# The multiplier of a gated recurrence, computed as (1 + a) times the root of -tanh(y/2) instead of through a reciprocal

## The reference

```python
r = sigmoid(gate_r(x)); i = sigmoid(gate_i(x))
log_a = -LRU_C * r * softplus(-lam)
a = exp(log_a)
mult = sqrt(-expm1(2.0 * log_a))          # the root of 1 - a^2
u = mult * (i * x)
h = scan(h = a * h + u)                   # along the 256 tokens
y_lru = h * gelu(u_g)
```

## Time and profile before

| | us |
|---|---|
| median of 3 runs | 942.52 |
| lowest and highest of them | 936.86, 943.32 |
| the profiled execution, its own time | 943.4 |
| its span, from the first to the last instruction | 941.6 |

### The profile page before, as it was taken

One profiled execution on the slowest core, in us unless ns is written; L12 is line 12 of the kernel. 1 busy time (PEld: TensorE's weight loads), 2 busy tenths in 40 slices (PEclk: granted clock), 3 DMA queues, 4 the chain that ended last, 5 costly groups with the idle time before them and its releaser, 6 DMA issues.

```text
span 941.6 us, 13290 instructions
## 1 busy us (share of the span) xinstructions
PE 811.3 (86%) x5425; PEld 644.0 (68%) x5425; DVE 506.0 (54%) x826; ACT 380.0 (40%) x629; POOL 44.4 (5%) x108
## 2 busy tenths in 40 slices
PE   6989997896686776659999997799999999999975
PEld 5967786763343332329989875487787999999854
DVE  5786547411110030055936988945677666666655
ACT  5563647210100100046456655535445544444444
POOL 5000020010101101000000000000000000000000
PEclk9998998998987889779999997989999999999988
DMA  9941181399999999995417452055554566665001
GB/s 285 374 153 45 46 334 46 139 409 422 422 422 420 420 422 421 410 333 170 149 64 302 160 202 89 1 201 179 179 179 134 185 193 196 189 191 200 11 0 45
DMA packets 75950, 205.81 MB, mean 219 GB/s; under 512 B 5720, under 2 KB 48896, under 8 KB 63600
## 3 DMA queue, kind: packets, MB, share of 16 engines
q1 hardware_dynamic: 67406, 150.44, 44.7%
q0 software_dynamic: 8480, 54.49, 14.3%
q10 hardware_dynamic: 2, 0.00, 0.0%
HBM read 203.87 MB, written 1.05 MB: 218 GB/s over the span
## 4 chain that ended last, share of the span: by engine, by line
PE 62%; DMA 16%; DVE 14%; ACT 4%; issue 2%; SPq 0%; POOL 0%; ACTq 0%; DVEq 0%
DMA big<-in_w_up 16%; PE ps L1938 8%; PE ps L1939 8%; PE ps L1940 8%; PE ps L1741 8%; PE ps L1743 7%; PE ps L1742 7%; PE ps L2052 4%; DVE WL L1069 2%; PE ps L2031 1%; DVE XT L1558 1%; DVE WL L1061 1%; DVE big L1600 1%; ACT WH L622 1%; PE ps L2066 1%
## 5 line engine op out<-in xcount | busy, mean ns | idle before, releaser
L1069 DVE TENSOR_TENSOR WL<-big,WH 128x1024 fp32r<-128x1024 f32 x154 | 186.8, 1224 | 111.8 <-ACT WH L622 110.2
L622 ACT ACTIVATE WH<-big 128x1024 fp32r<-128x1024 f32 x154 | 160.7, 1054 | 89.0 <-PE ps L1940 88.5
L1741 PE MATMUL ps<-XH,WH 128*128 128x256 f32 (+1 forms) x640 | 187.5, 293 | 1.0 <-DVE WL L1061 0.7
L1743 PE MATMUL ps<-XH,WL 128*128 128x256 f32 (+1 forms) x640 | 183.1, 286 | 0.0
L1742 PE MATMUL ps<-XL,WH 128*128 128x256 f32 (+1 forms) x640 | 183.1, 286 | 0.0
L1741 PEld LDWEIGHTS ps<-XH,WH 128*128 128x128 f32 x640 | 123.7, 193 | 6.6 <-issue 4.5
L2052 PE MATMUL ps<-big 128*32 128x256 f32 x1024 | 77.8, 470 | 55.1 <-DMA big<-in_w_gate 33.3
L1742 PEld LDWEIGHTS ps<-XL,WH 128*128 128x128 f32 x640 | 123.8, 194 | 0.8
L1743 PEld LDWEIGHTS ps<-XH,WL 128*128 128x128 f32 x640 | 123.6, 193 | 0.0
L2052 PEld LDWEIGHTS ps<-big 128*32 128x32 f32 x1024 | 42.8, 135 | 92.0 <-issue 81.9
L1938 PE MATMUL ps<-WH,XH 128*128 128x512 f32 x240 | 96.6, 402 | 5.6 <-DVE WL L1069 2.1
(11 more groups left out here) (399 smaller groups left out, 1091.7 us busy)
## 6 DMA issues: line engine op xcount, KB each, us to landing
big<-in_w_in SPq DMA_DIRECT2D x35, 1024.0 KB, 9.2
big<-in_w_gate SPq DMA_DIRECT2D x16, 1024.0 KB, 17.1
big<-in_w_up SPq DMA_DIRECT2D x16, 1024.0 KB, 18.2
big<-in_w_gate POOLq DMA_DIRECT2D x16, 1024.0 KB, 19.4
big<-in_w_up POOLq DMA_DIRECT2D x16, 1024.0 KB, 20.1
big<-in_w_down SPq DMA_DIRECT2D x16, 1024.0 KB, 18.6
big<-in_w_down POOLq DMA_DIRECT2D x16, 1024.0 KB, 21.2
big<-in_w_mlp_up SPq DMA_DIRECT2D x16, 1024.0 KB, 5.5
```

The costliest lines, as they stand in the source:

```text
L622: s.activation(dst, src, ACT.Copy).then_inc(ev("unit_high"), 1)
L1069: v.tensor_tensor(dst, src, h.bitcast(F32), ALU.subtract).then_inc(ev("unit_split"), 1)
L1741: mm(o, h, rh, start=first, stop=False, skip_group_check=skip)
L1743: return mm(o, l, rh, start=False, stop=last, skip_group_check=skip)
```

## The change

The reciprocal form is taken out. Tanh gets y/2 through its scale. DVE no longer computes the eight chunks of L1557 to L1559; instead, in steps 30 to 33, it multiplies the gated input by 1 + a, two chunks at a time. ACT's Sqrt of -t follows the Gelu immediately, in steps 33 and 34, and what comes after on DVE stands five steps earlier: the product with the root in steps 35 to 38, the scans in 39 to 42, the gated outputs in 40 to 43. No other engine's stream changes.

```diff
-                    s.activation(half_of(zc, k - 27), half_of(zx, k - 27), ACT.Tanh).then_inc(ev("tanh_done"), 1)
+                    s.activation(half_of(zc, k - 27), half_of(zx, k - 27), ACT.Tanh, scale=0.5)\
+                        .then_inc(ev("tanh_done"), 1)
...
-                if k in (38, 39):
-                    act.wait_ge(ev("one_minus_a2"), 4 * (k - 37))
-                    s.activation(half_of(zc, k - 38), half_of(zc, k - 38), ACT.Sqrt).then_inc(ev("mult_ready"), 1)
+                if k in (33, 34):
+                    s.activation(half_of(zc, k - 33), half_of(zc, k - 33), ACT.Sqrt, scale=-1.0)\
+                        .then_inc(ev("mult_ready"), 1)
...
-                if 29 <= k < 37:
-                    c = k - 29
-                    dve.wait_ge(ev("tanh_done"), 1 + c // 4)
-                    th_, xt = zc[:, c, :], XT[:, 0, 0:S]
-                    chain(v.tensor_scalar(xt, th_, -1.0, 1.0, ALU.mult, ALU.add))
-                    chain(v.reciprocal(xt, xt))
-                    v.scalar_tensor_tensor(out=th_, in0=th_, scalar=-2.0, in1=xt, op0=ALU.mult, op1=ALU.mult)\
-                        .then_inc(ev("one_minus_a2"), 1)
-                    dve.wait_ge(ev("one_minus_a2"), c + 1)
-                if 40 <= k < 44:
-                    q = k - 40
+                if 30 <= k < 34:
+
+                    q = k - 30
+                    dve.wait_ge(ev("a_ready"), 1 + q // 2)
+                    dve.wait_ge(ev("gated_input"), 4)
+                    v.scalar_tensor_tensor(out=two(zi, q), in0=two(zx, q), scalar=1.0, in1=two(zi, q), op0=ALU.add,
+                                           op1=ALU.mult).then_inc(ev("one_plus_a"), 1)
+                if 35 <= k < 39:
+                    q = k - 35
                     dve.wait_ge(ev("mult_ready"), 1 + q // 2)
-                    dve.wait_ge(ev("gated_input"), 4)
+                    dve.wait_ge(ev("one_plus_a"), 4)
                     v.tensor_tensor(two(zi, q), two(zi, q), two(zc, q), ALU.mult).then_inc(ev("lru_input"), 1)
-                if 44 <= k < 48:
-                    if k == 44:
+                if 39 <= k < 43:
+                    if k == 39:
                         dve.wait_ge(ev("lru_input"), 4)
-                        dve.wait_ge(ev("a_ready"), 2)
-                    for c in (2 * (k - 44), 2 * (k - 44) + 1):
+                    for c in (2 * (k - 39), 2 * (k - 39) + 1):
                         v.tensor_tensor_scan(out=zc[:, c, :], data0=zx[:, c, :], data1=zi[:, c, :], initial=0.0,
                                              op0=ALU.mult, op1=ALU.add).then_inc(ev("scanned"), 1)
-                    if k > 44:
-                        gated_output(k - 45)
-            gated_output(3)
+                if 40 <= k < 44:
+                    gated_output(k - 40)
             dve.wait_ge(ev("lru_done"), 4)
```

## The result

Over twelve runs of each, the changed kernel has a median of 934.49 us (933.05 to 937.94) against 942.09 (936.86 to 943.68). The ratio of the runs is 0.9930, with a 95% interval of 0.9916 to 0.9943: 6.6 us less, between 5.4 and 7.9. (The medians alone are 7.6 us apart, the means of the twelve 6.5.) In a second measurement, six runs against ten, it was 0.9929 (0.9904 to 0.9954). The forecast was 937.3 and a saving of 5.2 us, within 1%, in a range of 931.5 to 941.0.

The account below looks back on a forecast made before the run. PE, busy 86% of the span, waits for DVE's reciprocal steps in the token units and for a late first mask. Savings of 2.99 and 2.18 us sum to 5.2, taking the median 942.52 to 937.3, range 931.5 to 941.0.

Parts of the forecast that it names:

- What bounds the kernel: Token units: PE needs 21.96 us per eight units if nothing is late; DVE's reciprocal steps made the first half 2.99 longer.
- Point 1, the stalls: Token units: PE's three stalls on DVE's splits vanish, saving 2.99 us, with bounds of about 2.1 and 3.0.
- The sign named for DVE's time: Sign that the forecast is right: DVE's time over the whole 16 token units falls by about 17 us.
- Point 2, the scans: Steps 39 to 43: DVE falls about 1.6 us behind, covered by 5.9 to spare; cost nothing, at most 1.6 without cover.
- Point 3, ACT: Around units 36 to 38: the moved roots and table load cost nothing, since the smaller slack is 4.0 us.
- Point 4, the mask: Stage end: first mask starts 0.55 us behind the scores instead of 2.73, saving 2.18, bounds 1.9 and 2.7.
- The clock: PE's pause before the attention shrinks from 4.31 to about 2.1 us; whether the clock still falls was open, counted as nothing.
- the two terms: The forecast's two savings: 2.99 us from PE's stalls and 2.18 from the first mask, together 5.2 us.
- Rival A: Clock stays up over the shorter pause: 1.8 us in attention rounds, about 2 in the unit behind; 933.5 us; chance 0.15.
- B: Only one of the two terms comes, as stalls move elsewhere or the mask waits for something else: about 940 us; chance 0.11.
- C: Clock stays at 1.2 GHz through all the attention and first units behind: 6.1 us lost against 5.2 saved, 943.4; chance 0.04.
- D: The change doesn't reach the path; PE's idle time moves into the attention: 942.5 us; chance 0.02.

Follow-up runs that it names:

- idle reciprocals: Changed kernel plus eight idle tensor_scalar and reciprocal pairs on DVE in steps 29 to 36, nothing depending on them: 938.03 us, ratio to the kernel before 0.9956.
- copies: Changed kernel plus three or six idle 128 x 1024 copies on ACT between first root and unit 37's high part: 931.24 and 939.85 us, one run each.
- late tail: Changed kernel with scans and gated outputs back in steps 44 to 47 and behind the loop, new arithmetic kept: 938.24 us, ratio to the kernel before 0.9953.
- table ahead: Changed kernel plus a one-element Sigmoid on ACT behind the loop's last high part, loading the table before the mask: 932.94 us, ratio to the kernel before 0.9909.

## Why the prediction was right, and where it fell short

**What bounds the kernel.** Right. PE's 21.96 us for eight units without a late split was the measure of what could be had, and both halves came out at 21.88 and 21.89.

**Point 1, the stalls.** Forecast 2.99, measured 3.14 in the traces. The lower bound, the three idle times with 2.1 us together, was too low: the stretch lost 3.14. The new product takes 0.684 us in the mean of four, as taken (0.69). That the reciprocals' time caused the stalls is shown by the idle reciprocals, which bring 3.52 us back. The sign named for DVE's time, about 17 us less, holds from step 27 to the first mask: DVE is busy for 54.99 us from 510.00 to 573.78 before and for 38.47 from 509.03 to 567.53 after, 16.5 less. Within the token units alone it is 11.3, since the first of the eight steps lie ahead of them and the last gated outputs behind.

**Point 2, the scans.** Right: no wait of PE for a split among the scans, though the step with the copy runs late.

**Point 3, ACT.** The forecast had the split of unit 37 done 4.0 us before it is needed; the copies measure 3.8. No DMA became late: in the token units every idle time of ACT ahead of a high part ends with PE.

**Point 4, the mask.** Forecast 2.18 (0.55 us behind the scores), measured 2.14 (0.59). The late tail shows it apart from point 1.

**The clock.** I counted nothing for it, and this is where the sum may be short: the total is 6.6 us (5.4 to 7.9) against 5.3 in the two terms. The forecast's pause, 2.1, was right (2.18), but the clock fell in the attention all the same, only later: over the pause it is 1.00 now, and in the second trace 0.68 over the 54 us. Rival A supposed that it stays up. In the first trace its 3.8 us came about in sum (3.6 in two stretches) but not in its parts. The rounds gave 1.2 for the 1.8. The stretch with the first unit gave 2.4 for the 2.0, although only six matmuls of that unit, from 615.81 to 618.37, are slow in the kernel before, 1.2 us, and not ten; the rest is the last round's own work on PE, which also ran at half the clock. In the second trace the opposite of A came about. That the sum is near is luck.

Whether the shorter pause helps on average is not settled. For it: the mean granted clock over the whole run is 0.9412 over the 34 measured runs of three kernels with a short pause (12 and 6 of the changed kernel, 10 with idle reciprocals, 6 with the table ahead) and 0.9365 over the 44 with the long one (32 of the kernel before, 12 of the late tail), with a spread of some 0.0045 in single runs. Against it: the mean clock also contains the first attention, where the kernel before was slower in all its three traces for no cause that an edit gives, and in the traces the clock behind the short pause ranges from 0.68 to 0.94. The kernel with the late tail, whose pause is long, also gains 1.3 us beyond its term, and the one with idle reciprocals 2.4 beyond its own. So the shorter pause alone doesn't explain what lies beyond the two terms. It may come from the second attention, from the first, or from both, and stays open. The Trainium skill says in TensorE: Matmul & The Clock Gate, section What's actually happening, that the monitor behind the clock runs free of the kernel; the two traces of the changed kernel agree with it, 0.94 and 0.68 over the same 54 us of the same program.

**The other rivals.** B fell with the copies and the windows, C did not come about in the totals (though the second trace of the changed kernel shows that a single execution can lose 5.6 us against another in this way). C's price of 6.1 us was too high: that trace, the slowest of all behind the mask, takes 90.2 us there, 2.0 more than the first trace of the kernel before. D fell with the total, 6.6 us and clear of zero, and with the rows: the two terms came, and nothing behind them took them back.

## What to carry to other kernels

When an engine that prepares operands is not the busiest by far but stands on the chain in one stage, compare its time per step with the consumer's time per step in that stage; the excess, less the lead, is what the rewrite is worth. The lead need not be known: here eight units with late splits against eight without gave 3.0 of 20 us of removed work, measured 3.1. Look for the second gain at the stage's end, where work of the old stage stands in the stream ahead of the first instruction of the next; moving it was worth two thirds as much as the arithmetic, and a table load could follow it out of the way for another 1.3. Below 1%, split single traces at instructions that both kernels share before believing their difference.

## What the runs showed of the hardware that was not expected

- Two executions of one program differed by 5.6 us in 90, with a granted clock of 0.94 in the one and 0.68 in the other over 54 us, while the token units, at a clock of 1.00, repeated within 0.02 us in every trace with the same work (43.76 and 43.77; 46.91 and 46.93).
- The clock held at 1.00 over a pause of 4.32 us in the kernel with the late tail, and had a mean of 0.73, 0.88 and 0.87 over one of 4.31 or 4.32 in the three traces of the kernel before: the length of a pause alone did not tell when it fell.
- A change of function set on ACT cost its load only: load at 528.35, 1.28 us long, root at 529.65.
